# Gated attention's scores within a block: twelve products of 32 keys each, in place of five of 32 to 128

## The reference, cut to what matters

```python
qg = qc * jnp.exp(b)          # b: running sum of log gates in the chunk
kg = kc * jnp.exp(-b)
kd = kc * jnp.exp(b_last - b)
attn = jnp.where(causal, jnp.einsum('bhnid,bhnjd->bhnij', qg, kg), 0.0)
o_intra = jnp.einsum('bhnij,bhnjv->bhniv', attn, vc)
def step(state, xs):
    o_n = jnp.einsum('bhcd,bhdv->bhcv', qg_n, state)
    state = dec_n[..., None] * state + jnp.einsum('bhcd,bhcv->bhdv', kd_n, v_n)
```

## Time and profile before

| | |
|---|---|
| median of 3 runs | 918.63 us |
| profiled execution, its own time | 917.4 us |
| its span, first to last instruction | 915.6 us |
| PE busy (matmuls) | 898.0 us, 98% |
| PEld busy (weight loads) | 767.8 us, 84% |
| DVE busy | 494.4 us, 54% |
| ACT busy | 368.7 us, 40% |
| mean granted TensorE clock | 0.997 of full speed |

### The profile page before, as it was taken

The page is one execution under the profiler, slowest core; times in us unless marked ns, Lnnn a source line. Parts: engine busy times, 40 slices in busy tenths (PEclk is TensorE's granted clock), DMA queues, the critical chain, the costliest instruction groups (busy, mean ns, idle before and its releaser), DMA issues.

```text
span 915.6 us, 11818 instructions
## 1 busy us (share of the span) xinstructions
PE 898.0 (98%) x4635; PEld 767.8 (84%) x4635; DVE 494.4 (54%) x580; ACT 368.7 (40%) x461; POOL 35.9 (4%) x33
## 2 busy tenths in 40 slices
PE   6999999999999999999999999999999999999996
PEld 6998888889898988888888888888888888888885
DVE  6878875636462646542544476555555556422223
ACT  6541226593534365332223345333333334322235
POOL 0010000000000000000021210000000000000003
PEclk9999999999999999999999999999999999999998
DMA  9976745115251525452233431333333332332202
GB/s 326 301 240 165 191 98 157 48 47 184 92 185 47 184 93 184 144 179 92 80 119 133 129 93 47 92 94 105 107 106 92 92 92 92 121 109 92 92 0 92
DMA packets 117133, 112.91 MB, mean 123 GB/s; under 512 B 7412, under 2 KB 107126, under 8 KB 114663
## 3 DMA queue, kind: packets, MB, share of 16 engines
q1 hardware_dynamic: 116375, 110.21, 38.6%
q10 hardware_dynamic: 720, 2.16, 0.7%
HBM read 104.80 MB, written 4.21 MB: 119 GB/s over the span
## 4 chain that ended last, share of the span: by engine, by line
PE 92%; DVE 3%; SPq 2%; DMA 1%; issue 1%; ACT 0%; DVEq 0%; ACTq 0%
PE bank L1773 27%; PE bank L1774 26%; PE bank L1775 26%; DVE ada_in L1155 1%; PE bank L2280 1%; DMA ada_in<-in_ada_w_dram 1%; SPq L446 1%; PE bank L1917 1%; PE bank L1955 1%; PE bank L2045 1%; PE bank L2013 1%; PE bank L1912 1%; PE bank L1928 1%; PE bank L1889 1%; SPq L510 1%
## 5 line engine op out<-in xcount | busy, mean ns | idle before, releaser
L1773 PE MATMUL bank<-h_hi,w_hi 128*128 128x512 f32 x672 | 264.7, 394 | 0.0
L1775 PE MATMUL bank<-h_hi,w_lo 128*128 128x512 f32 x672 | 261.7, 389 | 0.0
L1774 PE MATMUL bank<-h_lo,w_hi 128*128 128x512 f32 x672 | 261.6, 389 | 0.0
L1775 PEld LDWEIGHTS bank<-h_hi,w_lo 128*128 128x128 f32 x672 | 126.1, 188 | 26.6
L1773 PEld LDWEIGHTS bank<-h_hi,w_hi 128*128 128x128 f32 x672 | 126.2, 188 | 25.9 <-issue 0.2
L1774 PEld LDWEIGHTS bank<-h_lo,w_hi 128*128 128x128 f32 x672 | 126.2, 188 | 25.4 <-issue 0.2
L1228 DVE TENSOR_TENSOR w_lo<-raw,w_hi 128x2048 fp32r<-128x2048 f32 (+2 forms) x44 | 81.0, 1854 | 86.9 <-ACT w_hi L673 86.9
L1235 DVE TENSOR_TENSOR w_lo<-raw,w_hi 128x2048 fp32r<-128x2048 f32 x31 | 71.1, 2293 | 86.3 <-ACT w_hi L681 86.3
L1727 DVE SCALAR_TENSOR_TENSOR conv<-bank,vecs,conv 128x511 f32<-128x511 f32 x88 | 65.7, 748 | 65.8 <-ACT conv L1087 60.3
L681 ACT ACTIVATE w_hi<-raw 128x2048 fp32r<-128x2048 f32 x31 | 59.1, 1906 | 69.3 <-PE bank L1775 69.3
L673 ACT ACTIVATE w_hi<-raw 128x2048 fp32r<-128x2048 f32 (+2 forms) x42 | 67.9, 1630 | 46.9 <-DMA raw<-in_w_in_dram 34.2
(11 more groups left out here) (282 smaller groups left out, 1253.7 us busy)
## 6 DMA issues: line engine op xcount, KB each, us to landing
raw<-in_w_up_dram SPq DMA_DIRECT2D x44, 512.0 KB, 5.0
raw<-in_w_in_dram SPq DMA_DIRECT2D x17, 1024.0 KB, 5.3
raw<-in_ada_w_dram SPq DMA_DIRECT2D x16, 1024.0 KB, 5.5
raw<-in_w_in_dram SPq DMA_DIRECT2D x22, 512.0 KB, 5.3
raw<-in_w_down_dram SPq DMA_DIRECT2D x22, 512.0 KB, 3.7
ada_in<-in_ada_w_dram SPq DMA_DIRECT2D x16, 512.0 KB, 9.5
raw<-in_w_gla_branch_dram SPq DMA_DIRECT2D x4, 1024.0 KB, 4.9
raw<-in_w_out_dram SPq DMA_DIRECT2D x4, 1024.0 KB, 5.0
```

What stands on the lines that cost most here:

```text
L1773: pe.matmul(out_ap, wh, xh, start=first, stop=False, skip_group_check=True)
L1774: pe.matmul(out_ap, wh, xl, start=False, stop=False, skip_group_check=True)
L1775: return pe.matmul(out_ap, wl, xh, start=False, stop=last, skip_group_check=True)
```

## The change

The scores of a block are now twelve products in place of five, and each has exactly 32 keys (32 weight columns) and writes the 32 partitions of PSUM that belong to its keys. The level of single chunks is eight products of 32 keys by 16 queries, the next two of 32 by 32, the last two of 32 by 64. Nothing is computed that a later product overwrites. Consecutive products write different groups of 32 partitions. The blocks are the outer loop now, the levels the inner one. VectorE's copies, the masks, the semaphores and the transposes are as before.

```diff
                 for b in range(NB):
-                    blk = slice(b * P, (b + 1) * P)
-                    queries = q_in[:, h % 2, blk].rearrange("p (n e c) -> p e n c", e=2, c=CHUNK)
-                    at = side[2][:, blk]
-                    at_chunks = at.rearrange("p (n e c) -> p e n c", e=2, c=CHUNK)
-                    for e, own in enumerate((k_in[:, h % 2, blk], mixed[:, blk])):
-                        pe.matmul(at_chunks[:, e], own, queries[:, e], start=True, stop=True, skip_group_check=True)
-                for o in (1, 0):
-                    m, col = 32 + 64 * o, 32 + 64 * o
-                    for b in range(NB):
-                        pe.matmul(side[2][0:m, b * P + col:b * P + col + 32], k32[:, b * P:b * P + m], q32[:, b, o, :],
-                                  start=True, stop=True, skip_group_check=True)
-                for b in range(NB):
-                    last = pe.matmul(side[2][0:P // 2, b * P + P // 2:(b + 1) * P], k64[:, b, :], q64[:, b, :],
-                                     start=True, stop=True, skip_group_check=True)
+
+                    def level(c, first, width, keys, queries):
+                        at = b * P + first
+                        return pe.matmul(side[2][32 * c:32 * (c + 1), at:at + width], keys, queries, start=True, stop=True,
+                                         skip_group_check=True)
+
+                    for e in range(2):
+                        own = (k_in[:, h % 2, :], mixed[:, :])[e]
+                        for c in range(4):
+                            at = b * P + 32 * c
+                            level(c, 32 * c + CHUNK * e, CHUNK, own[:, at:at + 32],
+                                  q_in[:, h % 2, at + CHUNK * e:at + CHUNK * (e + 1)])
+                    for c in (2, 0):
+                        level(c, 32 * (c + 1), 32, k32[:, b * P + 32 * c:b * P + 32 * (c + 1)], q32[:, b, c // 2, :])
+                    for c in (1, 0):
+                        last = level(c, P // 2, P // 2, k64[:, b, 32 * c:32 * (c + 1)], q64[:, b, :])
                 last.then_inc(at_ps, 1)
```

## The result

| | before | after |
|---|---|---|
| median | 918.42 us (917.99 to 919.01, 6 runs) | 910.34 us (909.52 to 911.49, 6 runs) |
| ratio to before | | 0.9912, 95% interval 0.9899 to 0.9925 |
| profiled execution, its own time | 917.4 us | 910.8 us |
| its span | 915.6 us | 909.0 us |

The change makes the kernel 8.1 us faster. I had forecast 919.5 us with a range of 917.0 to 923.9, and given 0.07 to "faster".

A forecast was written before the change was run, and what follows sets the result against it. TensorE was taken as the bound. Per head 3.47 us of new pairs plus 0.20 of seams replaced 3.45, +0.9 us over four heads; added to 918.63 this gave 919.5 us, range 917.0 to 923.9.

The forecast's parts named there:

- What bounds the kernel: TensorE's stream sets the time; a nanosecond gained or lost in `within` moves the end as much, four times.
- What one pair costs: Load plus matmul on TensorE costs the larger of load and stream: 5 ns plus 0.83 ns a column.
- the sum: Score stretch per head: removed and added pairs plus seams, 3.67 us against 3.45; +0.22 a head, +0.9 us in all.
- the value I picked inside my bounds for 64 columns on 32 weights: Score pairs of 32 weight columns with 64 streamed: 0.059 us each, taken from between 0.031 and 0.059.
- rival 3: Score stretch limited by instruction supply, +13.8 us (932.4), or by a falling granted clock, about as much; chance 0.06.
- I take no cost and no gain: At the 44 changes of column tile a head in the scores, nothing lost or gained; the sum stays +0.9 us.
- The bound from below: Whole score products hide behind neighbours on other tiles, 1.5 us a head, 6.1 in all; range end -5.2 us.
- rival 4: Loads or streams of different column tiles overlap in the scores; gain reaches 5.2 us (913.4); chance 0.08.
- the sum's own 0.20 of seams: Changes of tile width into and out of the 32-column score products, 0.20 us a head.
- The rivals on the slower side: Score tile changes: unhidden loads, +5.2 us, chance 0.13; full seams, +16.7 us, 0.04; or supply or clock limits, 0.06.

The follow-up runs named there:

- On one tile: Changed kernel with every score product writing partitions 0 to 31, other keys' scores left out; 918.79 us, ratio 1.0007 to the kernel before.
- the last-but-one version: Changed kernel with the one-column sums of ada_acc and of the last norm also put on four column tiles; 904.19 us, ratio 0.9854.
- the run tile by tile: Changed kernel's same 48 products a head, ordered with the column tile as outermost loop; 917.27 us, ratio 0.9992 to the kernel before.

## Why the prediction was wrong

**What bounds the kernel** was right. TensorE's stream sets the time: 4 x 2.03 us less in `within` is 8.1 us less in the medians. TensorE's waits add up to 10.3 us against 9.9, and the two new ones, of 0.4 us each, stand before the changed code.

**What one pair costs** was right. On one tile every term came out: 0.031 for 16 streamed columns, 0.057 for 64 (I had 0.059), and 3.76 us from the last projection product to the transposes where the sum says 3.79. (The stretch alone is 3.55, not 3.67: the seam into 32 columns falls ahead of line 2011's first start, 0.21 us behind the last projection product where it was 0.12.) So was the value I picked inside my bounds for 64 columns on 32 weights. The supply of instructions (rival 3) was never a limit: 0.0085 us a pair in the last-but-one version; the granted clock was 1.00 over `within`.

**The step that failed** is the last one of the sum: "I take no cost and no gain" at a change of column tile. The rows of before have no pair that follows one of another tile, and I filled the gap with the nearest row. That row is of pairs on one tile, which can't show it. What the runs show in its place: at such a change there is no seam and no bare load, but a second, third and fourth line. The term "no gain" should have been -2.2 us a head: 96 pairs take 1.33 us on four tiles and 3.55 on one. Against this I had argued that "all loads read through the same 128 rows, one after another in every row I have". One after another was an observation on one tile; that they must was my own addition. Loads to different tiles start 0.008 us apart.

**The bound from below was no bound.** I priced rival 4, the right mechanism, as a product that hides behind its neighbour, which is two lines. Four tiles are four lines, and the price follows from the work of the busiest: 0.31 us a block, 1.23 a head, and with the sum's own 0.20 of seams 1.43 us where 3.45 stood. Times four that is -8.1 us, what was measured, and every number of it is in the earlier trace rows. The 0.08 for this side should have been the largest chance, or at least one of the two largest.

A rule for it lay open. The Trainium skill, "TensorEngine Tiling (Array Packing)", section Key Properties, says besides the sentence on draining that I used that different tiles can execute weight loads and matmuls in parallel. I cited the half that left my sum as it was. The runs agree with both halves: a seam of 0.09 us at a change of width, and loads 0.008 us apart on different tiles. The Trainium skill, "TensorE: Matmul & The Clock Gate", Part 3, says in its list of what overlaps that a load overlaps only when its group of rows differs (its text above the list also lets a load into the background weight buffer go ahead). The runs disagree with that "only" here too, since all these products use all 128 rows.

**The rivals on the slower side** (1, 2 and 3) are refuted by the timeline after: the whole stretch of 1.33 us is less than half of what its 96 pairs cost on one tile, which leaves no room for a cost at 44 changes.

## What to carry to other kernels

Products with few weight columns and few streamed ones run on TensorE's column tiles side by side if each writes its own group of 32 partitions: price them by the busiest tile's own pairs, not by their sum, and put neighbours in the list on different tiles (runs of two fp32 products of one tile did no harm, whole chains lost nearly all). The first to look for are products whose cost is the load of 128 weight columns with a column or a few streamed. And where the trace lacks the very case the change brings in, the nearest row is no forecast: its bound has to come from how many units could work at once.

## What the runs showed of the hardware

- Column tiles of 32 and of 64 columns ran side by side in fp32, weight loads included: 0.014 us a pair in the changed kernel, 0.0085 where all four tiles are evenly loaded, 0.031 on one tile.
- How far TensorE looks past a pair that is held up: at all three changes of tile in the run tile by tile, a pair of the next tile started with three pairs of the tile ahead still to come, so matmuls start out of the list's order. Four pairs of one tile in a row cost 0.02 us a head, six 0.09, whole chains 1.8.
- A change of tile width costs about 0.09 us each way (0.21 in place of 0.12 us behind the last projection product); a change of tile at the same width costs nothing (1.33 us, where the busiest tile's own pairs are 1.23 and the seam out 0.09).
